# Moving weight tiles stored in reverse and read from the last column to the first, in a two-layer float32 trunk on one core

## The reference

```
for i in range(2):
    if i == 0: q, k, v = h @ w_qkv; m = softmax(causal(rope(q) rope(k)^T)) v @ w_o
    else:      y = groupnorm((rope(q) rope(k)^T * decay) v); m = (silu(h @ w_g) * y) @ w_o
    h = layer_norm(alpha * h + m)
    u = conv3(h @ w_in); g, val = split(u)
    h = layer_norm(alpha * h + (gelu(g) * val) @ w_out)
```

## Time and profile before

| quantity | value |
|---|---|
| time, median of 3 | 2647.94 us (2647.67 to 2648.49) |
| the profiled execution's own time | 2648.49 us |
| its span, first to last instruction | 2646.7 us |
| mean granted TensorE clock | 0.995 |
| TensorE matmuls, weight loads | 14368 and 14368 |
| HBM read | 490.70 MB |

### The profile page before, as it was taken

How to read it: one execution, slowest core, us unless ns; L and a number is a source line. 1 busy time by engine, 2 the same in 40 slices (tenths; PEclk the granted TensorE clock), 3 DMA queues, 4 the chain that set the end, 5 groups by cost and what they waited for, 6 DMA issues and landing times.

```text
span 2646.7 us, 40802 instructions
## 1 busy us (share of the span) xinstructions
PE 2612.0 (99%) x14368; PEld 2266.8 (86%) x14368; DVE 1600.4 (60%) x1842; ACT 1257.2 (48%) x1387; POOL 15.2 (1%) x38
## 2 busy tenths in 40 slices
PE   8999999999999999999999999999999999999998
PEld 8999888888888888888888888888788888888886
DVE  5666657666666654475555555554666666665455
ACT  4444435565656443334444444343365656554332
POOL 0000000000000000000000000000000000000000
PEclk9999999999999999999999999999999999999999
DMA  6545564555555565655555555566455555556654
GB/s 221 175 163 171 174 223 158 191 189 188 188 188 189 204 216 192 192 177 175 169 182 177 175 177 174 178 222 197 155 188 190 186 194 183 194 190 228 196 188 148
DMA packets 136978, 493.78 MB, mean 187 GB/s; under 512 B 15056, under 2 KB 17104, under 8 KB 135888
## 3 DMA queue, kind: packets, MB, share of 16 engines
q1 hardware_dynamic: 133136, 481.49, 55.1%
q10 hardware_dynamic: 3776, 11.37, 1.2%
HBM read 490.70 MB, written 2.10 MB: 186 GB/s over the span
## 4 chain that ended last, share of the span: by engine, by line
PE 98%; DVE 1%; DMA 0%; POOL 0%; issue 0%; ACT 0%; DVEq 0%; POOLq 0%; ACTq 0%
PE acc_ab L330 12%; PE acc_cm L330 12%; PE acc_ab L272 11%; PE acc_ab L274 11%; PE acc_ab L275 11%; PE acc_ab L333 6%; PE acc_cm L333 6%; PE acc_ab L289 5%; PE acc_ab L291 5%; PE acc_ab L293 5%; PE acc_cm L272 3%; PE acc_cm L275 3%; PE acc_cm L274 3%; PE acc_cm L356 1%; PE acc_cm L460 0%; DVE h L847 0%
## 5 line engine op out<-in xcount | busy, mean ns | idle before, releaser
L727 DVE TENSOR_TENSOR w_lo<-raw,w_hi 128x1024 fp32r<-128x1024 f32 x912 | 1105.8, 1223 | 838.2 <-ACT w_hi L507 835.2
L507 ACT ACTIVATE w_hi<-raw 128x1024 fp32r<-128x1024 f32 x912 | 948.7, 1055 | 882.7 <-PE acc_ab L275 469.7
L330 PE MATMUL acc_ab<-x_parts,w_hi 128*128 128x512 f32 x1408 | 493.7, 396 | 0.0
L330 PE MATMUL acc_cm<-x_parts,w_hi 128*128 128x512 f32 x1408 | 489.1, 394 | 0.0
L333 PE MATMUL acc_ab<-x_parts,w_lo 128*128 128x256 f32 x1408 | 391.4, 278 | 0.0
L333 PE MATMUL acc_cm<-x_parts,w_lo 128*128 128x256 f32 x1408 | 390.0, 277 | 0.0
L330 PEld LDWEIGHTS acc_ab<-x_parts,w_hi 128*128 128x128 f32 x1408 | 265.5, 189 | 61.3
L330 PEld LDWEIGHTS acc_cm<-x_parts,w_hi 128*128 128x128 f32 x1408 | 264.0, 188 | 61.3
L289 PE MATMUL acc_ab<-x_parts,w_hi 128*128 128x256 f32 x1024 | 295.8, 289 | 2.1 <-DVE w_lo L727 2.1
L291 PE MATMUL acc_ab<-x_parts,w_hi 128*128 128x256 f32 x1024 | 291.6, 285 | 0.0
L293 PE MATMUL acc_ab<-x_parts,w_lo 128*128 128x256 f32 x1024 | 291.6, 285 | 0.0
(11 more groups left out here) (111 smaller groups left out, 2839.2 us busy)
## 6 DMA issues: line engine op xcount, KB each, us to landing
raw<-in_weights_dram SPq DMA_DIRECT2D x912, 512.0 KB, 4.0
ln_gain<-in_ln_g_dram ACTq DMA_DIRECT2D x4, 1024.0 KB, 7.8
ln_bias<-in_ln_b_dram ACTq DMA_DIRECT2D x4, 1024.0 KB, 11.3
h<-in_x_dram SPq DMA_DIRECT2D x4, 512.0 KB, 8.4
decay_sb<-in_decay_tab_dram ACTq DMA_DIRECT2D x1, 1024.0 KB, 6.9
out_dram<-h SPq DMA_DIRECT2D x4, 256.0 KB, 2.5
out_dram<-h ACTq DMA_DIRECT2D x3, 256.0 KB, 2.5
conv_par<-in_conv_in_dram ACTq DMA_DIRECT2D x1, 352.0 KB, 11.4
```

Source lines behind the costliest of these rows:

```text
L330: pe.matmul(acc[:, f], w_hi[:, s % RING, k, c], x_parts[:, CK * s + k].rearrange("p a n -> p (a n)"), start=s == 0 and k == 0, stop=False, ...
L507: return act.activation(o, i, ACT.Copy)
L727: dve.tensor_tensor(w_lo[:, s], raw[:, s], w_hi[:, s].bitcast(F32), ALU.subtract).then_inc(lo_ready, 1)
```

## The change

Three things change, all of them in token-major products. The host stores every chunk that is used as the moving operand with its 512 columns in reverse (`turned_blocks`); the chunks used as the stationary operand stay as they were. In `multiply_tile` the moving operand is given by `backward`, an access pattern over the same 512 elements per partition that starts at the last and has a step of minus one. Reversed storage read in reverse gives the columns in their natural order, so PSUM holds what it held before, at the same places. No instruction is added, removed or moved, no wait changes, and the elementwise steps of ACT and DVE work on the chunk whatever the order of its columns.

```diff
+def backward(ap):
+
+    step, count = ap.ap[-1]
+    return bass.AP(ap.tensor, ap.offset + step * (count - 1), [*ap.ap[:-1], (-step, count)])
...
                 for k in range(CK):
-                    pe.matmul(o, xh[:, kt + k, c], wh[:, k], start=first and k == 0, stop=False,
+                    pe.matmul(o, xh[:, kt + k, c], backward(wh[:, k]), start=first and k == 0, stop=False,
                               skip_group_check=True)
-                    pe.matmul(o, xh[:, kt + k, c], wl[:, k], start=False, stop=False, skip_group_check=True)
-                    done = pe.matmul(o, xl[:, kt + k, c], wh[:, k], start=False, stop=True,
+                    pe.matmul(o, xh[:, kt + k, c], backward(wl[:, k]), start=False, stop=False, skip_group_check=True)
+                    done = pe.matmul(o, xl[:, kt + k, c], backward(wh[:, k]), start=False, stop=True,
                                      skip_group_check=True)
...
+def turned_blocks(w):
+
+    return column_blocks(w)[..., ::-1]
...
-    qkv = column_blocks(inp["moba_wqkv"][0])
+    qk, v = column_blocks(inp["moba_wqkv"][0][:, :2 * D]), turned_blocks(inp["moba_wqkv"][0][:, 2 * D:])
     for g in range(GROUPS):
-        parts += [qkv[g], qkv[GROUPS + g], qkv[2 * GROUPS + g]]
-    parts += list(column_blocks(inp["moba_wo"][0]))
+        parts += [qk[g], qk[GROUPS + g], v[g]]
+    parts += list(turned_blocks(inp["moba_wo"][0]))
...
-        return got + list(column_blocks(inp["ffn_w_out"][layer]))
+        return got + list(turned_blocks(inp["ffn_w_out"][layer]))
...
-    wv, wg = column_blocks(inp["ret_wv"][0]), column_blocks(inp["ret_wg"][0])
+    wv, wg = turned_blocks(inp["ret_wv"][0]), turned_blocks(inp["ret_wg"][0])
...
-    parts += list(column_blocks(inp["ret_wo"][0]))
+    parts += list(turned_blocks(inp["ret_wo"][0]))
```

## The result

The changed kernel takes 2690.05 us (median of 4 runs, 2680.51 to 2691.67) against 2647.81 us of the kernel before (2647.19 to 2648.49): a ratio of 1.0147, with a 95% interval of 1.0122 to 1.0171. It is 42.2 us slower. The likeliest case of the prediction was no change; the time lies inside the range.

What follows compares the result with a forecast made beforehand. TensorE was taken to bound the kernel, so matmul cost counts in full. The profiled 2648.5 us plus 0 for every term gave 2648.5 us, 2648 us for the median; range 2577 to 2720 us, same 0.57.

Steps and rivals of the forecast that it cites:

- What bounds the kernel, and the count: Whole kernel: TensorE is 98% of the chain; 5184 token-major matmuls take 1174.7 us, 44% of the span.
- The distance as the cost, split into columns and a rest: Token-major matmuls: 226.6 ns between starts, made of 512 columns at 0.416 ns and 13.4 ns left over.
- The host's reversal, ACT, DVE, loads: nothing: Chunk loads and elementwise steps: same bytes, 4.0 us loads, ACT 1.06 and DVE 1.23 us, so zero change.
- The moving operand's direction: Reader in all 5184 token-major matmuls: price taken as 0, bounded by 13.4 ns less and 213.8 ns more each.
- the prediction's own sign: Token-major matmul starts: the forecast counts as wrong if their distance is more than 1 ns from 226.6 ns.
- The rule on SBUF's lines: Moving operand's reads: full bandwidth while two successive accesses share a 16-byte line; four float32 still do, so price nothing.
- The fixed rest: Gap per matmul at full clock: the skill gives 2.5 ns, the trace 13.4; reaching the skill's figure would gain 56.5 us.
- Rival A: Moving operand's reader, token-major matmuls: half the columns per cycle when descending, 1038.9 us more, 3687 us; chance 0.17.
- Rival B: Start of each token-major stream: reader needs longer to begin, +13.4 ns each, 69.5 us more, 2718 us; chance 0.10.
- Rival C: Between token-major streams: the 13.4 ns left over shrink or go, up to 69.5 us less, 2578 us; chance 0.16.
- How fine a change would show: Whole-kernel measurement: about 0.2%, or 5.3 us, can be told from no change, 1.0 ns per token-major matmul.
- feature-major products as a sign of being wrong: Untouched feature-major products: a change in their own durations would show the prediction wrong; no reason seen for one.

Runs made afterwards that it cites:

- the clean pair of executions: Kernel before against one with only the read reversed, storage as before, both profiled with faster input products: span 2679.0 us, 32.3 us above before; that run's median 2691.61 us.
- the table of widths: Streams without the trunk, other engines idle, forwards and reverse at 128 to 512 columns: at 512, 226.7 ns forwards and 233.3 ns in reverse between starts.
- the bare kernel: Kernels without the trunk that stream only matmul forms, ACT, DVE and DMAs idle; 512 float32r columns take 226.7 ns forwards, 233.3 ns in reverse.
- four of a kind: Kernel before with four 512-column matmuls, then four 256-column ones, in the feed-forward input products instead of alternating: 2658.88 us, ratio 1.001.

## Why the prediction was right or wrong

- *What bounds the kernel, and the count.* Right. TensorE is 99% of the chain, the 5184 token-major matmuls are all there, and what each costs goes into the time one for one: 32.8 us in the sum of distances, 32.3 us between the spans of the clean pair of executions.
- *The distance as the cost, split into columns and a rest.* The distance was right, and it was the view that found the change's price; the lengths (389 to 397 ns) would have given 8 ns a matmul, not 6.3. The split is less than it looks. "The same is left at 256 columns" follows from the way the two numbers were made, out of two distances. By the table of widths, what a forwards stream takes beyond its columns at 2.4 GHz runs from 12 ns at 288 columns to 17 at 504, and is 13.4 at 512. In reverse it is 20.0 ns at 512.
- *The host's reversal, ACT, DVE, loads: nothing.* Right; the storage alone changed nothing, and the loads landed no later.
- *The moving operand's direction: "I take nothing".* This is the step that failed: a price was put at nothing, and the direction has one. By the prediction's own sign, a distance more than 1 ns from 226.6 ns, the forecast is wrong. The term measured 6.3 ns on average, 6.7 in a steady stream, between my bounds of -13.4 and +213.8 ns. The reasoning named the neighbours within a pair and within four, and that part was right: turned inside 16 bytes, the order is free (226.7 ns). It passed over the order in which the lines themselves come, and all of the price is there. I also wrote that the tile begins and ends on the same 2 KB boundary whichever way it is read, as if the place could not matter. The place does matter: the 226.7 ns of before are the best case of a rising stream, at 2 of 16 places in the bare kernel.
- *The rule on SBUF's lines* (the Trainium skill, SBUF — State Buffer, "Door 1: The DMA port swizzle") gives no price for the reverse, since four float32 of each line still follow each other. The runs show 6.7 ns, and the measurement decides. A step of two keeps two hits per line, and by the rule the full rate; the runs show 451 ns instead of 227.
- *The fixed rest* (the Trainium skill, TensorE: Matmul & The Clock Gate, "Back-to-back issue gap", 2.5 ns). In bfloat16 the bare runs agree with it, 215.8 ns for 512 columns of 213.3 ns. In float32r the rest is 13.4 ns forwards and 20.0 ns in reverse.
- *Rival A, half the rate.* Wrong. A step of two, where no columns are neighbours, takes 451 ns, as it would with a reader that serves pairs; but turned inside a pair or a line, the order costs nothing (226.7 ns).
- *Rival B, a longer start, 2718 us.* The right sign and half the size: 6.7 ns where I had put 13.4. Its mechanism isn't borne out. A start price would be there at 256 and 320 columns, and it isn't. That the time lies inside the range is owed to this rival's bound and not to the reasoning on the direction; it is luck as far as the mechanism goes.
- *Rival C, the rest goes.* Wrong; the rest grew.
- *How fine a change would show, and feature-major products as a sign of being wrong.* I took 0.2%, or 5.3 us, for what the measurement can tell. The runs of before alone spread over 20 us (2646.83 to 2667.29). A feature-major product did change, by 9.7 us in layer 1. It isn't the change's doing, since the same code runs at both speeds where no read is reversed (499.0 us in layer 0 in the trace of the storage alone, 490.2 in that of before), but the comparison's 42.2 us holds it. A second speed of an untouched stage was neither in the sum nor in the range.

What stays open is how the reader comes to need 6.7 ns more for a stream of falling lines. Shown are where it holds (float32r, or bfloat16 with a step of two; the full clock; falling order inside 256 bytes; most at 512 columns, none at 256 and 320) and what it isn't (storage, other engines, the use of one PSUM bank or four, one of two chance speeds). Two things aren't separated from it. A change of direction costs nothing to speak of in the trunk, but does where directions alternate in the bare kernel. And the place of the tiles and the length of the weight load move the forwards distance, so that the 6.7 ns are as much a rising stream's advantage in a good setting as a falling one's loss. That the two reads of SBUF, the moving stream and the next weight load, meet in banks of some kind is suggested by the 256 bytes and by the equal effect of 128 bytes on either tile, and is not shown.

## What to carry to other kernels

Where a float32r stream at the full clock bounds a kernel, read the distance between matmul starts against the column count, and treat the rest as a quantity that addresses can move: the order of 16-byte lines, and the place of the moving and the stationary tile within 256 bytes, each cost 5 to 7 ns per 512-column matmul here (1.2% of this kernel for the first). An edit that "only" shifts or turns a layout has to be priced through that rest, by a bare stream of the form in question; the bare streams here gave the trunk's numbers for the change, the shift of 128 bytes and the order of four of a kind. And before two medians are compared, compare the untouched stages of the two traces: 9.7 us of this difference belonged to one.

## What the runs showed of the hardware that I had not expected

- A float32r stream of 512 columns with neighbouring columns in turn takes 226.7 ns at the best place and 233.3 ns or more with falling lines. By place, direction and weight load all means lie between 226.7 and 240.0 ns, but for turned groups of 64 bytes, at 266.7 ns.
- Pairs of 512 and 256 columns settle into 346.7 or 353.3 ns after an idle stretch, with no cause found, and stay there for a whole stage of some 490 us. Four of a kind (350.8 ns a pair) and the alternating order (348.3 ns) have one speed.
- bfloat16 with a step of two costs about what float32r costs, 225.9 against 226.7 ns, and steps of 8 and 16 bytes cost 451 to 461 ns forwards alike.
- At the lower clock neither the rest nor the direction shows: 426.7 ns for 512 columns both ways.
